# A product-key expert layer: half of its token tiles on gathered rows, half against streamed tables

## The chip, the core and the metric

One core of a Trainium2 chip runs the whole program. Its engines work side by side and meet at semaphores: TensorE (PE, the products), VectorE (DVE), ScalarE (ACT), GpSimd (POOL) and SyncE (SP, which only issues transfers here); 16 DMA engines move the data. The metric is the device time of one execution in microseconds (us), the median of several runs.

## What is computed

A decoder block over 1024 tokens of width 1024, all in float32: attention (stick-breaking and sliding-window heads), then an expert layer with 16,384 experts. Each token picks 16 experts for each of 8 heads, 128 in all, and gets a sum of rows of `v`, weighted by a gate times a gelu of the dot product with the same rows of `u`:

```python
cand = (v1[..., :, None] + v2[..., None, :]).reshape(T, PEER_HEADS, PEER_TOPK * PEER_TOPK)
top_s, pos = lax.top_k(cand, PEER_TOPK)
idx = jnp.take_along_axis(cand_idx, pos, axis=-1)
gate = jax.nn.softmax(top_s, axis=-1)
h = jax.nn.gelu(jnp.einsum('cd,chkd->chk', xc, u[ic]))
return jnp.einsum('chk,chkd->cd', (gc * h).astype(v.dtype), v[ic])
```

`u` and `v` are 64 MiB each. A final normalisation follows.

## The kernel before

The 1024 tokens are 8 tiles of 128. The attention stages come first, with statically written loops; the change leaves them as they are. Then `experts` runs. `KeyScores` multiplies the normalised tokens (`x2_t`, stored transposed) with `w_q` and the keys, in two passes: tiles 0 and 1, then the other six; `evacuate` copies the scores out on ACT and SP stores them. DVE routes a tile (`pick_half_first` to `pick_gates`: two rounds of the best 8, on 16 sides of 128 scores and then on 8 tables of 256, the rows' numbers, the softmax), which gives 128 row numbers and gates for each token.

POOL then gathers: each indirect transfer (L1063) brings one 4 KB row for each of the 128 tokens, 512 KiB, into one of 8 slots for `u` or 8 for `v`. It stages 8 row numbers at a time (L1055). POOL's order is written out: the 128 gathers of `u` for tile 0; then, for each tile, groups of 8 of `v` for this tile and 8 of `u` for the next in turn; at the end the `v` rows of tile 7 alone. DVE takes the dot product of each gathered `u` row with its token (`dot_group`, L1197), 128 in a tile, with a part of the next tile's routing after every 16; `weigh` makes the weights. ACT turns each column of weights into a diagonal matrix (L1335), and PE multiplies it with the gathered `v` rows (`group`, L1372): two products of 512 columns for each gather. In tile 7 one `v` row in eight is added by DVE (`extra`). `finish` adds the residual and normalises.

Every engine runs its own list in order. A gather waits for its slot; a dot product or a product waits for its gather.

## Time and profile before

| | us |
|---|---|
| median of 3 runs | 4010.37 |
| lowest, highest | 4006.89, 4012.83 |
| the profiled execution (its span, first to last instruction) | 4053.9 |

The page gives busy time by engine, the chain of work that ended last, and groups of instructions by source line. Matrix products appear as MATMUL records; in float32 each product of the program leaves two records (the 128 products of 512 columns of L775 are 256 records). PEld is the load of the stationary operand.

### The profile page before, as it was taken

What the parts mean: (1) busy time and instruction counts of PE and PEld (TensorE: products, weight loads), DVE (VectorE), ACT (ScalarE), POOL (GpSimd) and SP (SyncE); (2) the same over time, 40 slices, a digit from 0 to 9 for tenths busy, and PEclk for the clock granted to TensorE, in tenths of its full rate; (3) what the DMA queues carried; (4) which work ended last, traced back from release to release, by engine and by line L of the source; (5) the groups of instructions that cost most, each with busy time, mean ns of one, the idle gap of its engine ahead of it and who ended that gap; (6) DMA issues with size and microseconds to landing.
All of it is one profiled execution on the core that took longest, in us unless ns stands there. A gap on an engine that the chain in (4) does not pass through costs nothing.

```text
span 4053.9 us, 36202 instructions
## 1 busy us (share of the span) xinstructions
PE 2946.8 (73%) x8280; PEld 1429.7 (35%) x8280; DVE 2097.3 (52%) x4538; ACT 704.7 (17%) x1566; POOL 2393.8 (59%) x2391
## 2 busy tenths in 40 slices
PE   8998978899056776666666676666766667666699
PEld 4655564566022232222222232222322223222243
DVE  1007872258856555654665465556645654444411
ACT  1116632111011111111111111111111111111122
POOL 1001004116777777777777777777777777777765
PEclk8999999999577888778887887878888788888899
DMA  3000012558899999999999999999999999999998
GB/s 104 32 0 1 1 47 85 166 167 298 286 369 324 358 370 348 347 348 360 354 357 346 370 345 348 353 374 334 353 351 381 335 343 356 365 354 356 354 334 304
DMA packets 352122, 1153.17 MB, mean 284 GB/s; under 512 B 36240, under 2 KB 80272, under 8 KB 351120
## 3 DMA queue, kind: packets, MB, share of 16 engines
q0 software_dynamic: 294912, 1073.87, 71.6%
q1 hardware_dynamic: 57104, 78.14, 5.6%
q8 instruction: 36, 0.59, 0.1%
q14 instruction: 70, 0.57, 0.0%
HBM read 1130.90 MB, written 20.97 MB: 284 GB/s over the span
## 4 chain that ended last, share of the span: by engine, by line
issue 27%; POOL 27%; PE 12%; DVE 8%; DMA 6%; POOLq 2%; DVEq 0%; ACT 0%; another core or an unknown queue 0%; SPq 0%; ACTq 0%
POOL ex_u L1063 14%; POOL ex_v L1063 11%; PE ex_acc L1372 10%; DMA ex_u<-in_peer_u,ex_index_u 4%; DMA ex_v<-in_peer_v,ex_index_v 2%; DVE ex_prod L1197 2%; PE kl_q L874 2%; DVE bias L1197 1%; POOL ex_index_v L1055 1%; DVE ex_left L1115 1%; DVE ex_half_i L1114 1%; POOLq L993 1%; DVE ex_half_v L1111 1%; POOLq L994 1%; POOL ex_index_u L1055 0%
## 5 line engine op out<-in xcount | busy, mean ns | idle before, releaser
L1372 PE MATMUL ex_acc<-ex_v,ex_diag 128*128 128x512 f32 x4032 | 2017.0, 664 | 1007.4 <-DMA ex_v<-in_peer_v,ex_index_v 768.5
L1372 PEld LDWEIGHTS ex_acc<-ex_v,ex_diag 128*128 128x128 f32 x4032 | 854.8, 215 | 2168.9 <-issue 2160.9
L1063 POOL DMA_INDIRECT ex_u<-in_peer_u,ex_index_u x1024 | 1114.3, 1088 | 385.4 <-issue 318.5
L1063 POOL DMA_INDIRECT ex_v<-in_peer_v,ex_index_v x1024 | 1066.7, 1042 | 414.5 <-issue 306.2
L1197 DVE CUSTOM_DVE_ANT_0 ex_prod<-ex_u,ex_x 128x1024 f32<-128x1024 f32 x512 | 628.7, 1228 | 1008.7 <-DMA ex_u<-in_peer_u,ex_index_u 878.2
L1335 ACT ACTIVATE ex_diag<-ident,ex_wt 128x128 f32<-128x128 f32 x1008 | 398.1, 401 | 2242.4 <-PE ex_acc L1372 1517.9
L1197 DVE CUSTOM_DVE_ANT_0 bias<-ex_u,ex_x 128x1024 f32<-128x1024 f32 x512 | 628.8, 1228 | 80.6 <-DMA ex_u<-in_peer_u,ex_index_u 53.2
L874 PE MATMUL kl_q<-x_t,ex_v 128*128 128x256 f32 (+1 forms) x768 | 228.3, 450 | 0.8 <-DVE keys_t L1254 0.8
L468 POOL TENSOR_SCALAR_AFFINE_SELECT st_sp<-st_sp 128x1024 f32<-128x1024 f32 x8 | 8.7, 1090 | 362.4 <-DVE st_sp L422 362.4
L252 PE MATMUL pj_acc<-x_t,pj_w 128*128 128x512 f32 x384 | 167.4, 599 | 1.3 <-DVE x_t L207 1.3
L874 PEld LDWEIGHTS kl_q<-x_t,ex_v 128*128 128x128 f32 x768 | 142.3, 190 | 66.4 <-issue 53.6
L415 DVE SCALAR_TENSOR_TENSOR x_t<-st_zs 128x1024 f32<-128x1024 f32 x36 | 45.4, 1262 | 142.6 <-ACT st_zs L371 142.4
L775 PE MATMUL mx_y<-qk_t,mx_mt 128*128 128x512 f32 x256 | 114.4, 605 | 3.7 <-ACT mx_mt L706 3.7
L252 PEld LDWEIGHTS pj_acc<-x_t,pj_w 128*128 128x128 f32 x384 | 73.7, 192 | 94.0 <-issue 92.3
L754 POOL TENSOR_TENSOR mx_hs<-mx_hs,minus_half 128x16 f32<-128x16 f32 x8 | 23.2, 2905 | 137.3 <-DMA mx_g<-in_norm_g 131.1
L325 PE MATMUL st_c<-st_sp,tri 128*128 128x512 f32 x144 | 79.4, 644 | 9.3 <-POOL st_sp L468 8.1
L1197 DVE DVE_READ_ACCUMULATOR2_ANT ex_dots<- 128x1 f32 x1024 | 84.1, 82 | 0.0
L1068 POOL TENSOR_TENSOR ex_index_ut<-ex_index,ex_zero_i 128x128 int32<-128x128 int32 x8 | 7.8, 979 | 126.7 <-DVEq L1189 124.3
L224 DVE COPY pj_w_twice<-pj_w 128x1024 f32<-128x1024 f32 x2 | 1.3, 690 | 145.9 <-DMA pj_w<-in_w_in 145.9
L775 PEld LDWEIGHTS mx_y<-qk_t,mx_mt 128*128 128x128 f32 x256 | 48.9, 194 | 64.5 <-issue 58.8
L249 PE MATMUL pj_acc<-pj_w,x_t 128*128 128x256 f32 (+1 forms) x384 | 69.9, 344 | 0.0
L1055 POOL TENSOR_TENSOR ex_index_v<-ex_index_vt,ex_zero_i 128x8 int32<-128x8 int32 x128 | 60.2, 470 | 11.9 <-PE ex_acc L1372 5.7
(162 smaller groups left out, 1930.2 us busy)
## 6 DMA issues: line engine op xcount, KB each, us to landing
ex_v<-in_peer_w_q SPq DMA_DIRECT2D x16, 1024.0 KB, 5.8
ex_u<-in_peer_u,ex_index_u POOLq DMA_INDIRECT x1024
ex_v<-in_peer_v,ex_index_v POOLq DMA_INDIRECT x1024
pj_w<-in_w_in SPq DMA_DIRECT2D x9, 1024.0 KB, 5.8
x_scratch<-mx_x SPq DMA_DIRECT2D x16, 512.0 KB, 2.7
ex_x<-x_scratch SPq DMA_DIRECT2D x16, 512.0 KB
ex_sc<-score_scratch SPq DMA_DIRECT2D x7, 1024.0 KB
mixed<-in_x SPq DMA_DIRECT2D x8, 512.0 KB, 4.1
```

The lines of the kernel that those rows point to most:

```text
L249: last = nc.tensor.matmul(acc[:, n % 4, 0:at[1]], h_t[:, c, part * P:(part + 1) * P], slot[:, c, at[0]:at[0] + at[1]], **st)
L252: last = nc.tensor.matmul(acc[:, n % 4, :], slot[:, c, at:at + P], h_t[:, c, part * HALF:(part + 1) * HALF], **st)
L325: last = nc.tensor.matmul(csum[:, cols], tri[:], soft[:, n % 3, cols], start=True, stop=kb == i)
L415: nc.vector.scalar_tensor_tensor(out=lsp[:, n % 2, :], in0=zs[:, n % 4, :], scalar=-1.0, in1=zs[:, n % 4, :], op0=ALU.mult, op1=ALU.max).t ...
L775: last = nc.tensor.matmul(y[:, t % 2, hf * HALF:(hf + 1) * HALF], m_t[:, t % 2, c, :], w[:, c, hf * HALF:(hf + 1) * HALF], start=c == 0, s ...
L874: last = self.nc.tensor.matmul(self.q[:, n % 2, 0:tiles * P], self.w[:, g % self.ring, c, (b % 2) * P:(b % 2 + 1) * P], self.x2_t[:, c, fi ...
L993: engine.wait_ge(signal, value)
L1055: nc.gpsimd.tensor_tensor(stage[:, half, :], tile_index[:, bass.ds(j * RG, RG)], zero_i[:, 0:RG], ALU.add).then_inc(ready, 1)
L1063: nc.gpsimd.indirect_dma_start(out=ring[:, k, :], out_offset=None, in_=table, in_offset=bass.IndirectOffsetOnAxis(ap=stage[:, half, k:k + ...
L1197: nc.vector.tensor_tensor_reduce(out=prod[k % 2][:], in0=u[:, k, :], in1=x2[:], scale=1.0, scalar=0.0, op0=ALU.mult, op1=ALU.add, accum_ou ...
L1335: nc.scalar.activation(diag[:, k, :], ident[:], ACT.Copy, scale=wt[:, bass.ds(j * RG + k, 1)]).then_inc(diag_ready, 1)
L1372: ins = nc.tensor.matmul(acc[:, hf * HALF:(hf + 1) * HALF], diag[:, k, :], v[:, k, hf * HALF:(hf + 1) * HALF], start=first and k == 0, sto ...
```

## The change

Tiles 0, 5, 6 and 7 (`PICKED`) keep gathered rows. Tiles 1 to 4 (`DENSE`) are computed against all 16,384 experts:

- `u`, laid out in advance as 128 chunks of 128 experts, transposed (`peer_ut`, a copy of the input in another order), and `v` are streamed by SP: for each chunk 512 KiB of each. `hidden` forms all dot products of a chunk with the live dense tiles (8 products of 128 columns for each live tile, in one instruction each); ACT applies gelu; `gated` multiplies with the gates on DVE; `values` multiplies with `v` (for each live tile 8 products of 512 columns in 4 chunks); `add` adds the result to a total in SBUF.
- The gates of a dense tile must be a full 128 experts by 128 tokens table for each chunk. `one_hots` (DVE) writes for four tokens the two one-hot patterns of their row numbers, `scale_ones` (4 ACT instructions) scales one by the gates, `build` (4 PE products of 128 columns) multiplies them, `read_gates` (ACT) copies the table out; there are 32 such batches for a tile. The table is stored to DRAM in rows of 512 bytes and loaded again, once per four chunks.
- The gathered tiles have 4 slots for `u` and 6 for `v`. The diagonals go. POOL's `spread` puts a token's 128 weights into one column of a 32-column operand otherwise zero, and `take` multiplies it with the 128 `v` rows of that token: four tokens at a time, in four column groups of 32, two halves of 512 columns, 8 products for 4 gathers. A `v` gather now brings the 128 rows of one token (so `index_v` is turned on PE).
- `schedule()` writes out 257 steps with work. A step has one chunk for the dense tiles that are live, and with it a number of dots, takes, routing pieces and gate batches. Routing is cut into 61 or 63 pieces, each of which waits for the one before it. The order in which tiles are routed is 0, 1, 2, 5, 3, 4, 6, 7.
- Nothing loops any more in this stage: all engines' lists are written out.

The diff, cut to its core:

```diff
+CHUNKS = 128
+SUB = 32
+BATCH = 4
+BLOCK = 4
+PICKED = [0, 5, 6, 7]
+DENSE = [1, 2, 3, 4]
+ROUTED = [0, 1, 2, 5, 3, 4, 6, 7]
...
+def schedule():
...
+        rate = {0: 2, 1: 2, 2: 2 if whole_team else 1, 3: 3 if whole_team else 2, 4: 4}
...
+        for _ in range(rate[n]):
+            g, at = dots // P, dots % P
+            if g >= len(PICKED) or k < routed_at.get(g, 1 << 30) + 2:
+                break
+            if at == 0 and g >= 1 and k < ended[g - 1] + 2:
+                break
+            if g >= 1 and at >= 10 and before[1] - 32 * (g - 1) <= (at - 10) // 4:
+                break
+            dots += 1
+            left -= 1.33
+            if at == P - 1:
+                ended[g] = k
+                break
+        s.dots = (first, dots)
+        start = taken
...
+        for _ in range(2 if n >= 3 else 1):
+            g, at = taken // 32, taken % 32
+            if g >= len(PICKED) or g not in ended or k < ended[g] + 4:
+                break
+            if g + 1 < len(PICKED) and before[0] - P * (g + 1) <= 4 * at + 2:
+                break
+            taken += 1
+        s.take = (start, taken)
...
-        u = sb("ex_u", [P, RG, D])
-        v = sb("ex_v", [P, RG, D])
-        diag = sb("ex_diag", [P, RG, P])
+        u = sb("ex_u", [P, RING, CH, NK])
+        v = sb("ex_v", [P, 2, GROUP, HALF])
+        a = sb("ex_a", [P, 2 * GROUP, ND * P])
+        gb = sb("ex_gb", [P, 2, ND * SUBS, BLOCK * SUB])
+        stage = sb("ex_stage", [P, CHUNKS, SUB])
...
+        stage = sb("ex_stage", [P, CHUNKS, SUB])
...
+        ru = sb("ex_ru", [P, USLOTS, D])
+        rv = sb("ex_rv", [P, VSLOTS, D])
...
+                def load_u(k):
+                    if k >= RING:
+                        sp.wait_ge(h_ready, k - RING + 1)
+                    sp.dma_start(u[:, k % RING, :, :], peer_ut[k % CHUNKS]).then_inc(u_in[k % RING], 16)
+
+                def load_v(b, half):
+                    if b >= 1:
+                        sp.wait_ge(v_done, half_done(b - 1, half))
+                    sp.dma_start(v[:, half, :, :], v_blocks[b % (CHUNKS // GROUP), half]).then_inc(v_in[half], 16)
...
+                def row_of_u(g, n):
+                    if n == 0:
+                        pool.wait_ge(picked, ROUTED.index(PICKED[g]) + 1)
+                    at = g * P + n
+                    if at >= USLOTS:
+                        pool.wait_ge(dot_done, at - USLOTS + 1)
+                    nc.gpsimd.indirect_dma_start(
+                        out=ru[:, at % USLOTS, :], out_offset=None, in_=peer_u,
+                        in_offset=bass.IndirectOffsetOnAxis(ap=index_u[:, g % 2, n:n + 1], axis=0)).then_inc(
+                            ru_full[at % USLOTS], 16)
+
...
+                def spread(g, q):
+                    at = g * 8 + q
+                    if q == 0:
+                        pool.wait_ge(wt_read, g + 1)
+                    if at >= 2:
+                        pool.wait_ge(taken, 4 * (at - 1))
+                    for i in range(4):
+                        n = 4 * q + i
+                        column = wt[:].rearrange("p (j s) -> p j s", s=32)[:, :, n:n + 1]
+                        last = nc.gpsimd.tensor_tensor(wm[:, at % 2, i], bcast(column, [P, 4, 32]),
+                                                       bcast(unit[:, 31 - n:63 - n].unsqueeze(1), [P, 4, 32]), ALU.mult)
+                    last.then_inc(wm_ready, 1)
+
+                def row_of_v(g, n):
+                    at = g * P + n
+                    if n == 0:
+                        pool.wait_ge(picks_read, ROUTED.index(PICKED[g]) + 1)
+                    if at >= VSLOTS:
+                        pool.wait_ge(taken, (at - VSLOTS) // 4 + 1)
+                    token = n % 4 * 32 + n // 4
+                    nc.gpsimd.indirect_dma_start(
+                        out=rv[:, at % VSLOTS, :], out_offset=None, in_=peer_v,
+                        in_offset=bass.IndirectOffsetOnAxis(ap=index_v[:, g, token:token + 1], axis=0)).then_inc(
+                            rv_full[at % VSLOTS], 16)
...
+                pool.wait_ge(ks.s_ready, UNITS)
+                for g in range(NG):
+                    for n in range(P):
+                        if n == 4 and g >= 1:
+                            root(PICKED[g - 1])
+                        if n % 16 == 0:
+                            spread(g, n // 16)
+                        row_of_v(g, n)
+                        if g + 1 < NG and n + USLOTS < P:
+                            row_of_u(g + 1, n + USLOTS)
+                        if g + 2 < NG and n + USLOTS >= P:
+                            row_of_u(g + 2, n + USLOTS - P)
...
+                def one_hots(d, i):
+                    b = d * BATCHES + i
+                    if i == 0:
+                        dve.wait_ge(picks_read, ROUTED.index(DENSE[d]) + 1)
+                    if b >= 2:
+                        dve.wait_ge(gp_full, b - 1)
+                    at = i * BATCH
+                    nc.vector.tensor_tensor(oh[:, b % 2, :, :, :],
+                                            bcast(iota[:].unsqueeze(1).unsqueeze(1), [P, 2, BATCH, NK]),
+                                            bcast(tr[:, d % 2, 0:2, at:at + BATCH].unsqueeze(3), [P, 2, BATCH, NK]),
+                                            ALU.is_equal).then_inc(oh_ready, 1)
...
+                def gated(k):
+                    lo, hi = live(k)
+                    b, c = k // GROUP, k % GROUP
+                    dve.wait_ge(gelu_done, k + 1)
+                    dve.wait_ge(gb_in[b % 2], 16 * (b // 2 + 1))
+                    if k >= 2 * GROUP:
+                        dve.wait_ge(v_done, half_done(b - 2, 1))
+                    cols = slice(lo * P, hi * P)
+                    nc.vector.tensor_tensor(a[:, k % (2 * GROUP), cols].rearrange("p (s t) -> p s t", t=SUB),
+                                            act_h[:, k % 2, cols].rearrange("p (s t) -> p s t", t=SUB),
+                                            gb[:, b % 2, lo * SUBS:hi * SUBS, c * SUB:(c + 1) * SUB],
+                                            ALU.mult).then_inc(a_ready, 1)
+
+                def add(n, half, d):
+                    dve.wait_ge(v_done, n + 1)
+                    if n == 0:
+                        dve.wait_ge(sums_in, 16 * ND)
+                    dest = total_of(d)[:, 4 * half:4 * half + 4, :]
+                    nc.vector.tensor_tensor(dest, whole(vp[:, n % 2, :]), dest, ALU.add).then_inc(added, 1)
...
+                for k in range(MORE):
+                    route(0, k)
+                for k in range(PIECES):
+                    route(1, k)
+                    if k == 4:
+                        move_index(0)
+                    if k % 6 == 5 and k >= 11:
+                        dot((k - 11) // 6) if k < 58 else None
+                for i in range(BATCHES):
+                    one_hots(0, i)
+                    for k in (2 * i, 2 * i + 1):
+                        if k < PIECES:
+                            route(2, k)
+                    if i % 2 == 1:
+                        dot(8 + i // 2)
+                for i in range(BATCHES):
+                    one_hots(1, i)
+                    dot(24 + i)
...
+                gated(0)
+                for k, s in enumerate(steps):
+                    if k >= 1:
+                        for n, b, half, d in values_at(k - 1):
+                            add(n, half, d)
+                    for g in s.done:
+                        add_rows(g)
+                    for g in s.weigh:
+                        weigh(g)
+                    for g in s.moved:
+                        move_index(g)
+                    for d, i in s.ones:
+                        one_hots(d, i)
+                    for at in range(*s.dots):
+                        dot(at)
+                    for n, piece in s.route:
+                        route(n, piece)
+                    if k >= 1:
+                        for t in [PICKED[g] for g in steps[k - 1].done] + [DENSE[d] for d in steps[k - 1].dense_done]:
+                            mean(t)
+                    if k >= 3:
+                        for g in steps[k - 3].done:
+                            scale(PICKED[g], x1[:], gf[:])
+                        for d in steps[k - 3].dense_done:
+                            scale(DENSE[d], total_of(d), whole(gf[:]))
+                    if k + 1 < TOTAL:
+                        gated(k + 1)
...
-                    for k in range(slots):
-                        pe.wait_ge(v_full[k], 16 * (t * GROUPS + j + 1))
-                        pe.wait_ge(diag_ready, at + k + 1)
-                        for hf in range(2):
-                            ins = nc.tensor.matmul(acc[:, hf * HALF:(hf + 1) * HALF], diag[:, k, :],
-                                                   v[:, k, hf * HALF:(hf + 1) * HALF],
-                                                   start=first and k == 0, stop=last and k == slots - 1)
-                        ins.then_inc(v_free, 1)
...
+                def hidden(k):
+                    lo, hi = live(k)
+                    cols = slice(lo * P, hi * P)
+                    at = slice((DENSE[0] + lo) * P, (DENSE[0] + hi) * P)
+                    pe.wait_ge(u_in[k % RING], 16 * (k // RING + 1))
+                    if k >= 2:
+                        pe.wait_ge(gelu_done, k - 1)
+                    for c in range(CH):
+                        last = nc.tensor.matmul(hp[:, k % 2, cols], u[:, k % RING, c, :], x2_t[:, c, at],
+                                                start=c == 0, stop=c == CH - 1)
+                    last.then_inc(h_ready, 1)
+
+                def values(n, b, half, d):
+                    if half == 0:
+                        pe.wait_ge(a_ready, GROUP * (b + 1))
+                    pe.wait_ge(v_in[half], 16 * (b + 1))
+                    if n >= 2:
+                        pe.wait_ge(added, n - 1)
+                    for c in range(GROUP):
+                        last = nc.tensor.matmul(vp[:, n % 2, :], a[:, (b * GROUP + c) % (2 * GROUP), d * P:(d + 1) * P],
+                                                v[:, half, c, :], start=c == 0, stop=c == GROUP - 1)
+                    last.then_inc(v_done, 1)
+
+                def take(n):
+                    g, s = n // 32, n % 32
+                    pe.wait_ge(wm_ready, 8 * g + s // 4 + 1)
+                    if s == 0 and g >= 1:
+                        pe.wait_ge(y_squared, turn_of[PICKED[g - 1]] + 1)
+                    for hf in range(2):
+                        for j in range(4):
+                            at = 4 * n + j
+                            if hf == 0:
+                                pe.wait_ge(rv_full[at % VSLOTS], 16 * (at // VSLOTS + 1))
+                            last = nc.tensor.matmul(gacc[32 * j:32 * j + 32, hf * HALF:(hf + 1) * HALF],
+                                                    wm[:, n // 4 % 2, n % 4, j, :],
+                                                    rv[:, at % VSLOTS, hf * HALF:(hf + 1) * HALF],
+                                                    start=s == 0, stop=s == 31, skip_group_check=True)
+                    last.then_inc(taken, 1)
...
+                turn_picks(ROUTED[0])
+                for d in range(BUILT_FIRST):
+                    turn_picks(DENSE[d])
+                    for i in range(BATCHES):
+                        build(d, i)
+                pe.wait_ge(ks.s_read, UNITS)
+                hidden(0)
+                for k, s in enumerate(steps):
+                    if k + 1 < TOTAL:
+                        hidden(k + 1)
+                    for t in s.turn:
+                        turn_picks(t)
+                    if k >= 1:
+                        for g in steps[k - 1].weigh:
+                            turn_weights(g)
+                    for d, i in s.build:
+                        build(d, i)
+                    for n in range(*s.take):
+                        take(n)
+                    for n, b, half, d in values_at(k):
+                        values(n, b, half, d)
...
+            a = _np.ascontiguousarray(a.reshape(CHUNKS, P, CH, P).transpose(0, 3, 2, 1))
```

## Rows read from the trace of the kernel before

**Rows 1.** The page: span and engines' busy shares.

```profile
span 4053.9 us, 36202 instructions
...
PE 2946.8 (73%) x8280; PEld 1429.7 (35%) x8280; DVE 2097.3 (52%) x4538; ACT 704.7 (17%) x1566; POOL 2393.8 (59%) x2391
```

**Rows 2.** Stage windows: busy us (x) per engine, PEclk, DMA share, GB/s.

```profile
800.00:1000.00 200.00, 199.50 (x793) 134.29 (x792) 139.01 (x470) 34.60 (x85) 72.23 (x64) 1.00 0.69 233
...
1700.00:2100.00 400.00, 270.24 (x539) 114.16 (x538) 224.36 (x521) 53.38 (x136) 294.83 (x301) 0.83 0.95 354
```

**Rows 3.** The page: the chain that ended last, by engine.

```profile
issue 27%; POOL 27%; PE 12%; DVE 8%; DMA 6%; POOLq 2%; DVEq 0%; ACT 0%; another core or an unknown queue 0%; SPq 0%; ACTq 0%
```

**Rows 4.** The page's groups: count, busy, mean ns, idle before, releaser.

```profile
L1372 PE MATMUL ex_acc<-ex_v,ex_diag 128*128 128x512 f32 x4032 | 2017.0, 664 | 1007.4 <-DMA ex_v<-in_peer_v,ex_index_v 768.5
...
L1063 POOL DMA_INDIRECT ex_u<-in_peer_u,ex_index_u x1024 | 1114.3, 1088 | 385.4 <-issue 318.5
...
L1335 ACT ACTIVATE ex_diag<-ident,ex_wt 128x128 f32<-128x128 f32 x1008 | 398.1, 401 | 2242.4 <-PE ex_acc L1372 1517.9
```

**Rows 5.** Timeline (start, us, engine, line): gathers, TensorE after a wait.

```profile
2014.17 0.94 POOL L1063 DMA_INDIRECT ex_v<-in_peer_v,ex_index_v  x1 [0.30 <-issue]
...
2014.79 15.79 PE L1372 MATMUL ex_acc<-ex_v,ex_diag 128*128 128x512 f32 x32 [14.54 <-DMA ex_v<-in_peer_v,ex_index_v]
...
2015.80 0.34 PEld L1372 LDWEIGHTS ex_acc<-ex_v,ex_diag 128*128 128x128 f32 x1 [0.52 <-issue]
2016.65 0.34 PEld L1372 LDWEIGHTS ex_acc<-ex_v,ex_diag 128*128 128x128 f32 x1 [0.52 <-issue]
```

**Rows 6.** A window before any gather: 512-byte score rows stored.

```profile
850.00:880.00 30.00, 29.50 (x120) 19.65 (x119) 28.39 (x86) 5.41 (x13) 0.00 (x0) 1.00 0.23 66
```

**Rows 7.** Timeline, key scores: products of 256, 128 and 512 columns.

```profile
781.33 3.62 PE L874 MATMUL kl_q<-x_t,ex_v 128*128 128x256 f32 x16
...
784.79 0.61 PE L884 MATMUL kl_s<-keys_t,kl_qt 128*128 128x128 f32 x4
...
832.03 7.03 PE L874 MATMUL kl_q<-x_t,ex_v 128*128 128x512 f32 x16
```

**Rows 8.** Timeline, stick-breaking stage: 64-column products, then what follows them.

```profile
401.21 1.09 PE L339 MATMUL st_o<-x_t,sb_v 128*64 128x128 f32 x16
402.23 1.16 PE L308 MATMUL st_z<-qk_t 64*128 64x128 f32 x16
```

**Rows 9.** Timeline: the first gather and its first reader.

```profile
885.78 1.20 POOL L1063 DMA_INDIRECT ex_u<-in_peer_u,ex_index_u  x1 [0.98 <-POOL ex_index_u L1055]
...
890.83 1.23 DVE L1197 CUSTOM_DVE_ANT_0 ex_prod<-ex_u,ex_x 128x1024 f32<-128x1024 f32 x1 [7.44 <-DMA ex_u<-in_peer_u,ex_index_u]
```

**Rows 10.** Groups after 820 us by shape: DVE, ACT and POOL.

```profile
L1239 DVE TENSOR_TENSOR ex_y<-ex_acc,ex_x 128x1024 f32<-128x1024 f32 x7 | 8.6, 1225 | 3.7 <-DVE ex_wt L1218 2.8 <-issue 0.9
...
L856 ACT ACTIVATE kl_out<-kl_s 128x512 f32<-128x512 f32 x16 | 9.6, 597 | 8.3 <-PE kl_s L884 6.3 <-issue 2.0
...
L1068 POOL TENSOR_TENSOR ex_index_ut<-ex_index,ex_zero_i 128x128 int32<-128x128 int32 x8 | 7.8, 979 | 126.7 <-DVEq L1189 124.3 <-issue 1.4 <-POOL ex_index_vt L1068 1.0
```

**Rows 11.** Timeline of tile 0's routing on DVE: three of its groups.

```profile
843.33 0.87 DVE L1120 MAX8 ex_half_v<-ex_left 128x8 f32<-128x128 f32 x4
...
846.08 2.77 DVE L1129 TENSOR_TENSOR ex_cand<-ex_half_v 128x256 f32<-128x256 f32 x8
...
883.10 0.29 DVE L1186 TENSOR_TENSOR ex_gates<-ex_gate_e,ex_gsum 128x128 f32<-128x128 f32 x1
```

**Rows 12.** Key scores: first and last start of products and early copies.

```profile
L874 PE MATMUL kl_q<-x_t,ex_v x725: 379/379/595, 779.8 to 1018.2; 128*128 128x256 f32 x118, 128*128 128x512 f32 x64
...
L853 ACT ACTIVATE ex_sc<-kl_s x15: 272/277/277, 781.5 to 839.6; 128x128 f32<-128x128 f32 x15
```

**Rows 13.** Timeline of the end: last sum and store.

```profile
4044.38 1.23 DVE L1239 TENSOR_TENSOR ex_y<-ex_acc,bias 128x1024 f32<-128x1024 f32 x1 [2.12 <-PE ex_acc L1372]
...
4050.87 0.34 SPq L1040 DMA_DIRECT2D out<-ex_y  x1
```

946 lines of the change are left out of this document (566 added, 380 removed).

## Prediction

> **What bounds the kernel now.** I read the page first for the shares of the whole span: no engine is full, PE 73%, POOL 59%, DVE 52% [rows 1]. The stage windows say why: the key scores end at about 1019 us with PE full, and from 1300 to 3700 us every window looks like the one shown, the DMA engines at 0.95 of their time and 354 GB/s, POOL at 295 of 400 us, PE at 270, DVE at 224 [rows 2]. The chain agrees: 27% POOL and 27% "issue" against 12% PE and 8% DVE [rows 3]. The group of gathers has 1.09 us busy and 0.38 us idle each, mostly issue, 1.46 together [rows 4]; alone an issue is 0.94 + 0.30 = 1.24 us [rows 5], so it is the transfers that set 1.46: 512 KiB in 1.46 us is 359 GB/s. 2048 gathers at 1.46 are 2990 us of the 4054. All else hides under them. The clock of PE is 0.83 in that stage [rows 2] because it waits some 14.5 us and then starts at the lower level, 0.85 us from one weight load to the next [rows 5] where full speed has 0.44.
>
> **What goes.** 1024 of 2048 gathers: 537 MB, at 1.46 us some 1495 us of DMA time. With them half of the dots (512 x 1.23 us), all 1008 diagonals and the staging. All of that but the gathers is hidden.
>
> **What comes, and what it costs alone.** Stepping through `schedule()`, the dense tiles join at chunks 0, 0, 64 and 88, so the tables are streamed for 216 chunks: 226 MB, plus 67 MB of gates out and in, in rows of 512 bytes. The one window with such rows and little else moves 66 GB/s at a share of 0.23, 287 at a full share [rows 6], against 354/0.95 = 373 for 4 KB rows.
>
> PE's full-speed prices: 16 records of 512 columns take 7.03 us, so a product is 0.87 us; of 256 columns 0.45 or less; of 128 0.22 [rows 7]. A dense tile costs 8 x 0.217 + 2 x 0.867 = 3.47 us in each chunk; 512 tile-chunks are 1775 us of PE. At four live tiles a step is 13.9 us, at three 10.4, at two 6.9, at one 3.5.
>
> The take is the unknown. The trace shows no 32-column groups, only groups of 64: 8 products of 128 columns (16 records) start 1.02 us ahead of what follows them, some 0.13 each with the changes of form at both ends, where a full-width one has 0.22 [rows 8]. So two run at once. If four do, a take is 2 x 0.87 + 0.2 = 1.9 us; if two, 3.7; if none, 7.1. I take 1.9, by the row with column groups, and keep the others as rivals.
>
> The Trainium skill, "TensorEngine Tiling (Array Packing)", section "Theoretical Speedup", gives up to 2 for groups of 64 and up to 4 for groups of 32. The row agrees with the first; nothing here shows the second. By the Trainium skill's figure a take would be 1.9 us, by a limit of two 3.7.
>
> DVE: a dot 1.23 us, an add over 512 columns of PSUM 0.61 (half of the 1.225 for 1024), a one-hot batch (1024 elements) 1.2 [rows 9, 10]. Routing: from the cut of 4 sides at 843.33 to the table at 846.08 are two pieces and a cast, and from there to the gates 37.3 us [rows 11]. Each of the 61 pieces adds a wait of about 0.15: some 66 us a tile, 1.08 a piece.
>
> A gather's slot: from issue to reader 5.05 us with nothing queued [rows 9]. POOL's product for `spread` has 0.98 us for 128x128 as nearest row [rows 10], so 1 us in each take; below nothing is excluded, since it is an added instruction.
>
> **The sum, by stages.**
>
> Start. The key scores end at 1019 us as before [rows 12]; the early scores are there at 840, tile 0 is routed by about 890. Then tile 1's routing stops at piece 4, in `move_index(0)`: it waits for a transpose that PE does behind all key scores. That is the first lost stretch. From 1020: 56 pieces and 8 dots, 72 us; tile 2's routing with 32 one-hot batches and 16 dots, 132; 32 batches with a dot each, 86 (DVE 2.5 us a batch, ACT about 2.5: four scalings at 0.40 [rows 4] and a read of 512 columns at 0.6 [rows 10]). The last table's store and load, 15. The steps begin at 1325 us. DMA engines and PE stand nearly idle for 300 us.
>
> Steps 0 to 63, two tiles: PE 6.9, DVE 1.2 + 4 x 1.08 + 0.6 + 0.35 and waits of 0.5, 7.2. In 20 of them two gate batches bring PE to 8.7. 44 x 7.3 + 20 x 8.9 = 500.
>
> Steps 64 to 87, three tiles, 24 batches, 11 takes: 250 + 21 + 21 of PE, and 20 for steps in which DVE is longer: 312.
>
> Steps 88 to 127, four tiles, a take and four dots: PE 13.9 + 1.9 = 15.8. DMA: 8 gathers (4.2 MB) and 1.05 MB at 373 GB/s are 14.1, gates 0.9: 15.0, at the share of 0.95 15.8 too. Two limits at once; I take 16.4 for 38 steps: 655.
>
> Steps 128 to 191, two tiles, two dots and half a take: PE 7.9; DMA 3.15 MB and gates 8.9, at 0.95 9.4. DVE's rows must come two steps ahead, so I take 9.7: 621.
>
> Steps 192 to 215, one tile: PE 4.4, DMA 8.6/0.95 = 9.1, taken as 9.4: 226. Steps 216 to 221, gathers alone at 1.46 and `spread`: 38.
>
> Steps 222 to 256: 32 takes with nothing beside them. Six slots hold a take of four rows and two more; rows seven and eight are issued when a take ends: 0.2 + 1.24 to the second issue + 5 to its landing + 1.7 us of products (3.4 at the lower clock, which TensorE has after a wait, as in [rows 5]) = 8.1 to 9.8. At 9.0, and 14 to get the weights across: 302. The gathers alone would need 5.8.
>
> End: from the last sum to the last store were 6.5 us plus the store [rows 13]; now five tiles are finished there: 22.
>
> 1325 + 500 + 312 + 655 + 621 + 226 + 38 + 302 + 22 = 4001 us, against 4053.9: 53 less. The profiled execution is 1.1% above the median; 4001 less 1.1% is 3958. **So 1495 us of gathers are removed, and nearly all of it comes back**: about 300 in a start that is serial on DVE, 200 and more of streaming, and a stage of four tiles at PE's pace.
>
> **The rivals.**
>
> Slots too few (slower). In the stage with four tiles a take frees four `v` slots, and eight gathers of 1.4 us follow it in POOL's order; DVE, in order, stands at the dot of the fourth row, and with it the gated products and adds behind it. It decides from the point at which those gathers, beside the streams, take longer than a step: 15.8 of 16.4 us is my estimate of both. For it: the DMA share of 0.95 in the window [rows 2]. Against: 10 us of slack between a take and the next dot. Price: 2.2 us in 40 steps, 1.5 in 88, 1 in the last 32, 10 us at the start: 262 us, which gives 4263, as a run 4217.
>
> Two column groups at a time, not four (slower): 1.8 us more in 37 + 11 takes, hidden under DMA in the next 88 steps, 1.8 in the last 32: 144, a run of 4101. None at a time: 5.2 x 80, and 64 x 0.9: 474, a run of 4427.
>
> All hides well (faster): streams and gathers mix without loss, so steps 88 to 127 take 15.8, the next 88 take 9.0, the last 32 take 7.5, and the first 64 follow PE. That is 25 + 62 + 50 + 15 = 150 less, a run of 3810. For it: POOL's 0.30 us between issues may shrink without the extra semaphore instructions, and at 1.24 it was not the limit.
>
> **How the numbers follow.** My forecast 0.42, good hiding 0.20, slots 0.20, two groups 0.13, none 0.05. The likeliest case has its own range of 3890 to 4030, a fifth of which lies above 4002. The range reaches from 3800 to 4190: below it lies half of the good case, above it half of the slots' and the serial take. About 0.2% (8 us) is what a measurement here can tell. Faster: 0.20 + 0.42 x 0.78 = 0.53; same 0.05; slower 0.42.
>
> **What would show it.** The start: DVE's wait of about 100 us before 1019, and a first `hidden` product followed by a gap until 1325. The take: 16 records in 1.9 or 3.7 us. The stage with four tiles: step of 16.4 us, PE's share above 0.93 and clock near 1.0; were it DVE waiting on `ex_ru` and PE's share below 0.88, the slots rival is right. Steps 128 to 215: a DMA share at 0.9 or more with PE at 0.8 and then 0.5. The last takes: one in 9 us at 230 GB/s. The prediction is wrong if a resource that I left out sets the step, ACT above all (at four tiles it has only 0.6 us of gelu and so should be free), or if the written-out lists cost time of their own.

## The result, and the profile after

| | us |
|---|---|
| before, median of 19 runs (lowest, highest) | 4016.64 (4006.89, 4026.63) |
| after, median of 19 runs (lowest, highest) | 4007.39 (3996.77, 4020.39) |
| ratio, 95% interval | 0.9974, 0.9964 to 0.9985 |
| the profiled execution of after, its span | 4014.06, 4012.3 |

The changed kernel is 0.26% faster; the interval lies below 1, but by little. The forecast was 3958 us, 1.3% faster. The page of after, with span, busy shares, PE's 40 slices and its clock, the two large queues, the chain by engine, and four groups:

```profile
span 4012.3 us, 34704 instructions
...
PE 3402.4 (85%) x12844; PEld 1867.3 (47%) x12844; DVE 1787.3 (45%) x3894; ACT 639.9 (16%) x1413; POOL 1275.5 (32%) x1232
...
PE   7998978899257999899889999999998999665554
...
PEclk8999988999655999999999999999999999887776
...
q0 software_dynamic: 147456, 536.94, 37.2%
q1 hardware_dynamic: 268656, 369.67, 26.8%
...
PE 52%; DMA 18%; DVE 6%; POOL 2%; issue 2%; ACT 1%; SPq 0%; DVEq 0%; ACTq 0%; POOLq 0%
...
L1750 PE MATMUL ex_hp<-x_t,ex_u 128*128 128x256 f32 (+3 forms) x3456 | 938.4, 426 | 52.0 <-DMA ex_u<-in_peer_ut 52.0
L1761 PE MATMUL ex_vp<-ex_v,ex_a 128*128 128x512 f32 x2048 | 932.3, 602 | 3.2 <-DVE x_t L1536 2.5
...
L1340 POOL DMA_INDIRECT ex_rv<-in_peer_v,ex_index_v x512 | 526.7, 1029 | 528.9 <-PE ex_gacc L1775 402.7
L1775 PE MATMUL ex_gacc<-ex_rv,keys_t 128*32 128x512 f32 x2048 | 458.3, 729 | 257.2 <-DMA ex_rv<-in_peer_v,ex_index_v 256.7
```

PE has risen from 73% to 85% and POOL has fallen from 59% to 32% [rows 1]; the chain, which was 27% POOL and 27% "issue" [rows 3], is now 52% PE and 18% DMA. PE's slices have two thin places, one a quarter of the way in (2, 5) and one at the end (6 6 5 5 5 4). The windows by stage (start:end, length, then busy us and count for PE, PEld, DVE, ACT and POOL, PE's clock, DMA share, GB/s) put numbers on them:

```profile
1020.00:1100.00 80.00, 9.96 (x49) 8.54 (x47) 72.81 (x261) 6.86 (x20) 9.17 (x9) 0.54 0.37 110
1100.00:1240.00 140.00, 85.23 (x335) 74.14 (x334) 128.64 (x292) 75.64 (x211) 37.31 (x27) 0.50 0.58 177
1340.00:1840.00 500.00, 470.42 (x1780) 317.46 (x1779) 356.16 (x997) 104.29 (x274) 65.80 (x64) 0.99 0.69 235
1840.00:2160.00 320.00, 283.09 (x977) 145.95 (x976) 191.35 (x475) 55.62 (x146) 117.36 (x110) 0.95 0.79 279
2160.00:2800.00 640.00, 631.07 (x1892) 257.74 (x1891) 283.02 (x471) 28.30 (x48) 353.29 (x347) 0.99 0.91 333
2800.00:3400.00 600.00, 553.21 (x2083) 315.87 (x2083) 221.45 (x389) 25.75 (x68) 301.34 (x285) 0.96 0.95 352
3700.00:4012.00 312.00, 173.75 (x460) 29.38 (x460) 7.97 (x11) 5.74 (x10) 117.98 (x141) 0.70 0.60 198
```

Before, one window stood for the whole stage, with the DMA engines at 0.95 and PE at 270 of 400 us [rows 2]. Now there are different limits one behind the other: DVE from 1020 on (73 of 80 us, 129 of 140), PE from 1340 to 2800 (631 of 640 with four tiles), to 3400 the DMA engines by their share (0.95), with PE close behind (553 of 600), and nothing at all in the last 312 us: PE 174, POOL 118, DMA 0.60.

### The profile page after: what moved, and what is told of

It is laid out like the page before. It is cut to its first block, busy times and chain, and to the rows that moved or that the text cites. A ratio compares the mean times of both kernels' runs of the same rounds, so it can differ in the third digit from the quotient of the medians.

```text
span 4012.3 us, 34704 instructions
## 1 busy us (share of the span) xinstructions
PE 3402.4 (85%) x12844; PEld 1867.3 (47%) x12844; DVE 1787.3 (45%) x3894; ACT 639.9 (16%) x1413; POOL 1275.5 (32%) x1232
## 2 busy tenths in 40 slices
DMA packets 416279, 908.82 MB, mean 227 GB/s; under 512 B 26096, under 2 KB 188912, under 8 KB 415216
## 4 chain that ended last, share of the span: by engine, by line
PE 52%; DMA 18%; DVE 6%; POOL 2%; issue 2%; ACT 1%; SPq 0%; DVEq 0%; ACTq 0%; POOLq 0%
PE ex_vp L1761 18%; PE ex_hp L1750 16%; DMA ex_rv<-in_peer_v,ex_index_v 9%; PE ex_gacc L1775 7%; PE ex_hp L876 6%; DMA ex_u<-in_peer_ut 5%; PE ex_gp L1738 3%; DMA gate_scratch<-ex_stage 2%; DVE ex_ru L1509 1%; POOL ex_rv L1340 1%; POOL ex_ru L1315 1%; DVE ex_oh L1496 1%; ACT ex_stage L1641 1%; PE ex_vp L886 1%; DMA ex_ru<-in_peer_u,ex_index_u 0%
## 5 line engine op out<-in xcount | busy, mean ns | idle before, releaser
L1315 POOL DMA_INDIRECT ex_ru<-in_peer_u,ex_index_u x512 | 585.9, 1144 | 1441.2 <-DVE ex_hid L1509 1195.0
L1750 PE MATMUL ex_hp<-x_t,ex_u 128*128 128x256 f32 (+3 forms) x3456 | 938.4, 426 | 52.0 <-DMA ex_u<-in_peer_ut 52.0
L1761 PE MATMUL ex_vp<-ex_v,ex_a 128*128 128x512 f32 x2048 | 932.3, 602 | 3.2 <-DVE x_t L1536 2.5
L1750 PEld LDWEIGHTS ex_hp<-x_t,ex_u 128*128 128x128 f32 x3456 | 641.8, 195 | 384.8 <-issue 225.3
L1509 DVE CUSTOM_DVE_ANT_0 ex_ru<-ex_ru,ex_x 128x1024 f32<-128x1024 f32 x512 | 619.1, 1229 | 270.6 <-DMA ex_ru<-in_peer_u,ex_index_u 255.6
L1340 POOL DMA_INDIRECT ex_rv<-in_peer_v,ex_index_v x512 | 526.7, 1029 | 528.9 <-PE ex_gacc L1775 402.7
L1775 PE MATMUL ex_gacc<-ex_rv,keys_t 128*32 128x512 f32 x2048 | 458.3, 729 | 257.2 <-DMA ex_rv<-in_peer_v,ex_index_v 256.7
L1761 PEld LDWEIGHTS ex_vp<-ex_v,ex_a 128*128 128x128 f32 x2048 | 383.8, 193 | 499.3 <-issue 485.0
L1775 PEld LDWEIGHTS ex_gacc<-ex_rv,keys_t 128*32 128x32 f32 x2048 | 82.5, 120 | 577.4 <-DMA ex_rv<-in_peer_v,ex_index_v 400.7
L1738 PE MATMUL ex_gp<-ex_oh 128*128 128x128 f32 x1024 | 204.1, 363 | 124.0 <-ACT ex_stage L1641 84.3
L876 PE MATMUL ex_hp<-x_t,ex_rv 128*128 128x256 f32 (+1 forms) x768 | 228.3, 450 | 0.8 <-DVE keys_t L1558 0.8
```

The lines of the kernel that those rows point to most:

```text
L876: last = self.nc.tensor.matmul(self.q[:, n % 2, 0:tiles * P], self.w[:, g % self.ring, c, (b % 2) * P:(b % 2 + 1) * P], self.x2_t[:, c, fi ...
L1315: nc.gpsimd.indirect_dma_start(out=ru[:, at % USLOTS, :], out_offset=None, in_=peer_u, in_offset=bass.IndirectOffsetOnAxis(ap=index_u[:, g ...
L1340: nc.gpsimd.indirect_dma_start(out=rv[:, at % VSLOTS, :], out_offset=None, in_=peer_v, in_offset=bass.IndirectOffsetOnAxis(ap=index_v[:, g ...
L1509: nc.vector.tensor_tensor_reduce(out=rows, in0=rows, in1=x2[:], scale=1.0, scalar=0.0, op0=ALU.mult, op1=ALU.add, accum_out=hid[:, g % 2, ...
L1738: last = nc.tensor.matmul(gp[:, j, :], oh[:, b % 2, 1, j, :], oh[:, b % 2, 0, j, :], start=True, stop=True)
L1750: last = nc.tensor.matmul(hp[:, k % 2, cols], u[:, k % RING, c, :], x2_t[:, c, at], start=c == 0, stop=c == CH - 1)
```

## The stages, forecast and measured

Stage times from the starts of the `hidden` products of each chunk and of the takes (L1750, L1775). The columns "after" and "repeat" are two profiled executions of the same kernel, 4012.3 and 4005.4 us.

| stage | forecast | after | repeat |
|---|---|---|---|
| up to the first `hidden` | 1325 | 1296.6 | 1296.8 |
| steps 0 to 63 | 500 | 505.7 | 507.5 |
| steps 64 to 87 | 312 | 333.3 | 335.2 |
| steps 88 to 127 | 655 | 638.6 | 633.0 |
| steps 128 to 191 | 621 | 604.4 | 599.7 |
| steps 192 to 214 | 217 (of 226 for 24) | 209.4 | 209.5 |
| from step 215 to the last store | 371 (9, 38, 302, 22) | 424.3 | 423.7 |
| span | 4001 | 4012.3 | 4005.4 |

The sum of spans was right within 11 us, in part by luck: the last stage and steps 0 to 87 came out 80 us longer than forecast, the others 69 us shorter. What made the forecast miss came behind the sum.

## The experiments

Ratios are to the kernel before on the same chip, with 95% intervals. The two kernels with short dots and the last one ran on another chip than the rest; the kernel before takes 4020.75 us there, against 4017.03 and 4018.65.

### The same two kernels again

Both kernels unchanged, to see how far one profiled execution stands for its kernel.

> The kernel before, unedited, to have its profiled execution beside its times. Theory one: the execution of 4053.9 us on which the sum of the prediction was built was itself an outlier of about 1% above this kernel's runs; then this one lies within 0.3% of the median, 4005 to 4030. Theory two: the profiler slows this kernel's gathers, in every profiled execution; then it is 4045 to 4060 again, while the times of the runs stay at 4010 to 4020.

> The changed kernel, unedited, on the same chip as the kernel before. Both theories: span of 4000 to 4020 and a ratio of 0.996 to 0.999. The stages should stay within 1%: 639 us for steps 88 to 127, 604 for 128 to 191.

Measured: before 4016.68 us (0.9999, 0.9987 to 1.0011), span 4013.1; after 4006.91 (0.9975, 0.9960 to 0.9991), span 4005.4. A run's time is its span plus some 1.8 us in both (4014.91 for 4013.1, 4007.15 for 4005.4). The execution of before that the prediction was made from, 4053.9 us, lies above all 19 runs of that kernel, of which the highest is 4026.63. Its windows compared with the second one's show a stage that ran 1.4% slower all along: from 1300 to 3500 us 354 against 359 GB/s, and 1458 gathers against 1478. So it was an unusual execution. The durations from which the sum was made are the same in both (a dot has 1.228 us in either, a gather alone 0.94), so taking 1.1% off it was the error.

### One term each

**Tile 0's row numbers moved later.** In tile 1's routing the copy of tile 0's row numbers stands at piece 49 instead of piece 4.

```diff
-                    if k == 4:
+                    if k == 49:
                         move_index(0)
```

> Edit: the row numbers of tile 0 are taken over (move_index(0)) after piece 49 of tile 1's routing instead of after piece 4. Theory: in the changed kernel DVE waits 91.6 us there for a transpose that PE does behind all key scores, and everything after it is a serial start. 45 pieces at 1.08 us and 7 dots then run before 1020 us: the first product of the steps comes 50 to 56 us earlier than 1297 us, and the whole is 50 to 56 us shorter than the changed kernel (4012 us in the profile), so about 3958. Rival: the start hides behind something later (the gate tables' stores, the streams) and less than 15 us are won.

Measured: 3958.35 us (0.9862, 0.9832 to 0.9891). DVE's timeline of after, with the wait in brackets; then of this kernel, and its window behind the key scores:

```profile
1023.77 0.29 DVE L1487 CAST ex_index_v<-ex_tp 128x128 int32<-128x128 f32 x1 [91.64 <-PE ex_tp L1720]
```

```profile
1024.07 1.22 DVE L1458 TENSOR_REDUCE ex_row<-ex_cand 128x64 f32<-128x1024 f32 x1 [40.49 <-PE ex_tp L1720]
...
1020.00:1100.00 80.00, 37.63 (x156) 32.44 (x154) 71.28 (x222) 30.31 (x87) 14.22 (x9) 0.54 0.44 131
```

The wait of 91.64 us is the one that the prediction named (about 100 us). 45 pieces of routing, 49 us at 1.08, now run inside it, and 40.49 us are left. PE has 38 us of gate products in the window in which it had 10, and the first `hidden` starts at 1248.8 instead of 1296.6: 48 us, which is the whole gain of 49.

**More slots for the last takes.** From tile 5 on, the `v` gathers have ten slots: the six, and four in `ex_stage`, which holds gates until the last dense tile has stored them. An excerpt:

```diff
+WIDE = 10
...
+        def slot_of(at):
+            if at < P:
+                return rv[:, at % VSLOTS, :], (rv_full[at % VSLOTS], at // VSLOTS + 1)
+            s = (at - P) % WIDE
+            before = (P - s + VSLOTS - 1) // VSLOTS if s < VSLOTS else 0
+            rows = rv[:, s, :] if s < VSLOTS else rows_more[:, s - VSLOTS, :]
+            return rows, (rv_full[s], before + (at - P) // WIDE + 1)
```

> Edit: from tile 5 on the v gathers have 10 slots, the 6 of before and 4 in the gate staging buffer, which is free by then. Theory: in the last 32 takes the period of 10.1 us is a loop (take ends, two gathers issued, 5.2 us to land, 3.4 us of products at the lower clock) that exists only because four rows of each take are not prefetched. With 10 slots it falls to the larger of POOL (4 x 1.24 us and 1.1 of spread, 6.1) and DMA (4 x 1.46, 5.8): 6.2 us, 125 us less in all; steps 88 to 215 within 10 us of the changed kernel's 639 + 604 + 209. Rival one: the period is set by PE at its lower clock, it stays above 8.5 and less than 50 us are won. Rival two: slots also hold up steps 88 to 215, which then shorten by 40 us or more.

Measured: 3848.78 us (0.9583, 0.9564 to 0.9602). First the timeline of after in its last takes, then one window of after and of this kernel, and the gathers of this kernel in it:

```profile
3808.92 0.94 POOL L1340 DMA_INDIRECT ex_rv<-in_peer_v,ex_index_v  x1 [5.09 <-PE ex_gacc L1775]
3810.16 0.94 POOL L1340 DMA_INDIRECT ex_rv<-in_peer_v,ex_index_v  x1 [0.30 <-issue]
...
3815.44 3.81 PE L1775 MATMUL ex_gacc<-ex_rv,keys_t 128*32 128x512 f32 x14 [0.92 <-DMA ex_rv<-in_peer_v,ex_index_v]
...
3819.04 0.94 POOL L1340 DMA_INDIRECT ex_rv<-in_peer_v,ex_index_v  x1 [5.46 <-PE ex_gacc L1775]
```

```profile
3700.00:3820.00 120.00, 71.30 (x192) 12.25 (x192) 0.00 (x0) 0.00 (x0) 47.28 (x55) 0.72 0.62 205
```

```profile
3700.00:3820.00 120.00, 101.60 (x358) 17.70 (x356) 0.00 (x0) 0.00 (x0) 92.94 (x111) 1.00 1.01 396
...
L1358 POOL DMA_INDIRECT ex_rv<-in_peer_v,ex_index_v x55 | 51.6, 939 | 16.3 <-issue 15.4 <-PE ex_gacc L1794 0.9
```

With six slots the loop closes on itself: the first issue at 3808.92 and the next at 3819.04 are 10.1 us apart, made of 1.24 to the second issue, 5.28 until its landing starts the products (3810.16 to 3815.44) and 3.60 from there to the next issue. With ten, the releaser of POOL's idle time is no longer `ex_gacc` but "issue", the DMA engines move 396 GB/s at a share of 1.01, PE is back at full clock, and the last 31 takes last 171.1 us instead of 313.7, 5.5 us each. That is 143 of the 158 us; 9 to 14 lie in steps 128 to 191. The expectation had 6.2 us a take and 125 us in all: it priced `spread` at 1.1 us a take, and the trace has 0.4 (four products of 0.4 us for four takes). In the window a gather comes every 1.32 us, and POOL's own list (0.94 and 0.30 a gather, 0.10 of `spread`) is as long; whether the transfers, at a share of 1.01, would allow less wasn't tried.

**Two column groups instead of four.** The rows j and j+2 of a take share a column group, so two rows' sums are added onto the other two's and only two groups are in use.

```diff
-                            last = nc.tensor.matmul(gacc[32 * j:32 * j + 32, hf * HALF:(hf + 1) * HALF],
+                            last = nc.tensor.matmul(gacc[32 * (j % 2):32 * (j % 2) + 32, hf * HALF:(hf + 1) * HALF],
```

> Edit: the four tokens of a take are put into two column groups of 32 instead of four, so two tokens share one group and their sums are mixed (not the reference's output). Theory: the changed kernel runs four groups at once (starts 7 ns apart), a take of 1.9 us at the full clock. With two groups it is 3.6: 48 takes beside three or four dense tiles cost 1.7 us more each, 80 us, steps 128 to 215 stay, and the last takes go from 10.1 to 11.8: 135 us in all. Rival: PE has slack in steps 88 to 127 (DMA sets them), and the increase there stays under 30 us.

Measured: 4145.31 us (1.0325, 1.0302 to 1.0349). Two takes in the stage with four tiles, of after and then of this kernel (start, us, engine, line, operation):

```profile
2410.35 1.92 PE L1775 MATMUL ex_gacc<-ex_rv,keys_t 128*32 128x512 f32 x16
2426.13 1.93 PE L1775 MATMUL ex_gacc<-ex_rv,keys_t 128*32 128x512 f32 x16
```

```profile
2403.00 3.63 PE L1775 MATMUL ex_gacc<-ex_rv,keys_t 128*32 128x512 f32 x16
2420.49 3.63 PE L1775 MATMUL ex_gacc<-ex_rv,keys_t 128*32 128x512 f32 x16
```

A take is 1.92 us and 3.63 us: four at once, and two. The step shown grows from 15.78 to 17.49 us, by 1.71, the whole difference of the take. Over steps 88 to 127 it is 52 us (690.8 for 638.6; 58 against the repeat) for 37 takes, 1.4 to 1.6 each, so in this stage PE sets the step nearly alone. In steps 128 to 191, with half a take each, 64 x 0.85 = 54 us more of PE cost only 7 (12 against the repeat): PE had about that much slack, and is now busy 641 of the 660 us from 2800 to 3460. In the last takes, with nothing beside them, the price is 45 us.

**A quarter of the streamed `u`.** After the first three chunks only 2 of the 8 parts of each chunk are loaded; the products read what lies in the other six.

```diff
+                    part = CH if k < RING else 2
-                    sp.dma_start(u[:, k % RING, :, :], peer_ut[k % CHUNKS]).then_inc(u_in[k % RING], 16)
+                    sp.dma_start(u[:, k % RING, 0:part, :], peer_ut[k % CHUNKS][:, 0:part, :]).then_inc(u_in[k % RING], 16)
```

> Edit: after the first three chunks each load of u brings only 2 of the 8 parts of a chunk (128 instead of 512 KiB), so the dense tiles' sums are not the reference's; every instruction and wait stays. Theory: steps 128 to 215 are bound by the DMA engines (share 0.95), so 393 KB less in a step at 373 GB/s save 1.05 us: step of 9.44 goes to 8.4, of 9.1 to 8.0, 90 us in all; steps 88 to 127 are bound by PE and stay within 8 us of 639. Rival: the steps are bound by the slots and the order of DVE and POOL, and less than 30 us are won.

Measured: 3954.62 us (0.9848, 0.9831 to 0.9865). Steps 128 to 191 take 571.3 us instead of 604.4 (599.7 in the repeat), steps 192 to 214 200.9 instead of 209.4, steps 88 to 127 630.4 instead of 638.6 (633.0). The window of steps 128 on:

```profile
2800.00:3400.00 600.00, 562.00 (x2190) 322.28 (x2189) 232.78 (x412) 27.03 (x73) 322.45 (x308) 0.96 0.91 328
```

Transfers alone as the bound would have given some 90 us; 50 came, 37 to 42 of them after step 128, with the DMA share down only from 0.95 to 0.91. So the transfers do set part of the pace after step 128, and something else stands close behind. PE is one such thing (562 of 600 us here), the dots, which hold the gathers (below), another.

### What bounded the kernel before

The prediction read the DMA share of 0.95 as the bound of before. Two kernels test that, and the trace shows the mechanism.

**Half the bytes.** The kernel before with gathers of 2 KB instead of 4 KB rows, in the same number. Dots, products and the extra row read that half twice, so the sums are of other data.

```diff
-                            out=ring[:, k, :], out_offset=None, in_=table,
+                            out=ring[:, k, 0:HALF], out_offset=None, in_=table.rearrange("e (h n) -> (e h) n", h=2),
...
-                        nc.vector.tensor_tensor_reduce(out=prod[k % 2][:], in0=u[:, k, :], in1=x2[:], scale=1.0, scalar=0.0,
+                        nc.vector.tensor_tensor_reduce(out=prod[k % 2][:].rearrange("p (h n) -> p h n", h=2), in0=u[:, k, 0:HALF].unsqueeze(1).to_broadcast([P, 2, HALF]), in1=x2[:].rearrange("p (h n) -> p h n", h=2), scale=1.0, scalar=0.0,
```

> The kernel before with gathers of half a row (2 KB instead of 4 KB, 128 rows as before); dots and products read the half row twice, so the number of instructions and their shapes stay and the output is not the reference's. It asks what bound the kernel before. Theory of the prediction: the transfers set 1.46 us for each gather; with half the bytes POOL's own list is left, 8 x 1.24 us and the staging of 8 row numbers, 0.47 + 0.81 + 0.3, so 1.40, and only 0.06 to 0.1 x 1800 = 100 to 190 us go: 3830 to 3910. Rival: POOL's issues were themselves held up by full rings (1.09 busy against 0.94) in a way that the sum does not show, and the time falls under 3800.

**Short dots.** The kernel before with every dot over 8 instead of 1024 columns.

```diff
-                        nc.vector.tensor_tensor_reduce(out=prod[k % 2][:], in0=u[:, k, :], in1=x2[:], scale=1.0, scalar=0.0,
+                        nc.vector.tensor_tensor_reduce(out=prod[k % 2][:, 0:8], in0=u[:, k, 0:8], in1=x2[:, 0:8], scale=1.0, scalar=0.0,
```

> The kernel before with dot products over 8 of 1024 columns (not the reference's output); every instruction and wait stays, only DVE's long operation with two inputs goes. It asks what sets the 1.49 us of a gather there, after half the bytes have saved nothing. Theory: POOL's own list does, and its gathers are held while DVE runs a dot: in the trace of the kernel before those with a dot over less than a tenth of their time have 0.97 us, those with one over more than half 1.20. Without the long dots the mean falls from 1.06 to 0.95-0.97, the period to 1.38 to 1.42 and the time by 0.08 to 0.1 x 2048 = 130 to 200 us: 3820 to 3890. Rival: the DMA engines set it (share 0.96), the period stays at 1.46 or more and less than 60 us go.

Measured: half the bytes 4158.6 us (1.035, 1.033 to 1.0369), slower; short dots 3773.42 (0.9383, 0.9366 to 0.94), 247 us faster. The window from 1300 to 3500 us and two of POOL's groups in it (count, busy us, mean ns, idle before, releasers), first of the second execution of before, then of half the bytes, then of short dots:

```profile
1300.00:3500.00 2200.00, 1497.59 (x2948) 632.15 (x2949) 1259.47 (x2870) 303.41 (x772) 1640.84 (x1674) 0.82 0.96 359
...
L1063 POOL DMA_INDIRECT ex_u<-in_peer_u,ex_index_u x736 | 784.1, 1065 | 274.9 <-issue 195.9 <-POOL ex_index_u L1055 74.4 <-PE ex_acc L1372 4.6
...
L1055 POOL TENSOR_TENSOR ex_index_v<-ex_index_vt,ex_zero_i 128x8 int32<-128x8 int32 x92 | 51.9, 564 | 4.6 <-POOL ex_index_ut L1068 3.1
```

```profile
1300.00:3500.00 2200.00, 1413.11 (x2785) 594.72 (x2784) 1206.60 (x2768) 286.65 (x728) 1674.38 (x1582) 0.81 0.60 173
...
L1063 POOL DMA_INDIRECT ex_u<-in_peer_u,ex_index_u x699 | 825.2, 1181 | 259.1 <-issue 185.1 <-POOL ex_index_u L1055 70.3 <-PE ex_acc L1372 3.7
...
L1055 POOL TENSOR_TENSOR ex_index_v<-ex_index_vt,ex_zero_i 128x8 int32<-128x8 int32 x88 | 65.3, 742 | 3.9 <-POOL ex_index_ut L1068 2.6
```

```profile
1300.00:3500.00 2200.00, 1631.00 (x3223) 688.38 (x3224) 492.85 (x2980) 330.73 (x840) 1588.95 (x1825) 0.85 1.01 391
...
L1063 POOL DMA_INDIRECT ex_u<-in_peer_u,ex_index_u x806 | 760.9, 944 | 301.3 <-issue 212.0 <-POOL ex_index_u L1055 80.8 <-PE ex_acc L1372 7.6
...
L1055 POOL TENSOR_TENSOR ex_index_v<-ex_index_vt,ex_zero_i 128x8 int32<-128x8 int32 x100 | 21.4, 214 | 4.8 <-PE ex_acc L1372 1.6 <-POOL ex_index_ut L1068 1.5
```

With half the bytes the DMA engines fall to 0.60 and nothing gets faster, and with short dots the same bytes move 6% faster, so the share of 0.95 was not the bound. Both results lie outside their expectations: half the bytes were to save 100 us or more, short dots 130 to 200. With short dots the gathers of `u` take 0.944 us instead of 1.065, and the staging product for `v` 0.214 instead of 0.564 (the one for `u` has 0.21 in both). In the second execution of before the hold can be seen directly (start, us, engine):

```profile
2118.93 0.95 POOL L1063 DMA_INDIRECT ex_u<-in_peer_u,ex_index_u  x1 [0.30 <-issue]
2120.00 1.23 DVE L1197 CUSTOM_DVE_ANT_0 ex_prod<-ex_u,ex_x 128x1024 f32<-128x1024 f32 x1 [12.66 <-DMA ex_u<-in_peer_u,ex_index_u]
2120.18 1.86 POOL L1063 DMA_INDIRECT ex_u<-in_peer_u,ex_index_u  x1 [0.30 <-issue]
```

The gather at 2120.18 is issued into a running dot and ends 0.81 us after the dot does (2122.04 and 2121.23). So do the others: of the 1478 gathers in the window some 350 start with more than 0.2 us of a dot still to go, and nearly all of them end 0.81 us after its end. A gather that starts in no dot has 0.94 us for the most part, even where a dot begins during it. The account closes. From 1300 to 3500 us there are 1478 gathers in before, one in 1.488 us, and 1612 with short dots, one in 1.365. Of the 0.123 us less, 0.100 are the gathers' own length (1.055 to 0.955 on average over `u` and `v`), 0.022 the staging, 0.00 the idle time between them. 2048 x 0.123 = 252 us; the gain is 247. With short dots the DMA share reads 1.01, at 391 GB/s, but POOL's idle time is still "issue" and its own staging, and its gathers are at the length of one alone; that the transfers are the bound then is possible and not shown.

The Trainium skill, "SBUF — State Buffer", section "SBUF: two separate sides", says that a VectorE instruction with two SBUF inputs and a GpSimd instruction that reads SBUF exclude each other for the length of the whole instruction. The trace agrees: a gather issued into a dot waits for the dot's end, as above, and on average this costs a gather 0.10 us here.

Half the bytes made the kernel slower by the same hold. Its dots last the same 1.228 us, and gathers issued into one again end 0.82 us after it; but they are issued earlier in it, with 0.22 us of a dot still to go on average over all gathers, against 0.15 in before. A gather has 1.127 us on average instead of 1.055, and the staging for `v` 0.742 instead of 0.564, which is together the 0.09 us by which a gather's period is longer in this window (1.576 for 1.488). Why gathers and dots fall together in this way when the rows land sooner wasn't looked into.

**Short dots in the changed kernel.** The same edit at L1509.

```diff
-                    rows = ru[:, at % USLOTS, :]
-                    nc.vector.tensor_tensor_reduce(out=rows, in0=rows, in1=x2[:], scale=1.0, scalar=0.0, op0=ALU.mult,
+                    rows = ru[:, at % USLOTS, 0:8]
+                    nc.vector.tensor_tensor_reduce(out=rows, in0=rows, in1=x2[:, 0:8], scale=1.0, scalar=0.0, op0=ALU.mult,
```

> The same edit in the changed kernel (dots over 8 columns, not the reference's output). Theory: steps 88 to 127 are bound by PE and steps 128 to 215 by the DMA engines, where 0.52 us of gathers' holding do not matter; 639 and 604 + 209 us stay within 10 and 25 us; only the start, which is serial on DVE, gets shorter, by 56 dots x 1.15 = 64 us less what ACT holds up, 30 to 64 us. Rival: DVE's waits for gathered rows and its dots hold the steps; then steps 88 to 215 get 60 us or more shorter.

Measured: 3930.57 us (0.9772, 0.9746 to 0.9797), 76 us less than the changed kernel on the other chip, and 82 by the spans (3923.0 for 4005.4). The window of steps 128 on:

```profile
2800.00:3400.00 600.00, 552.35 (x2216) 318.52 (x2215) 90.97 (x423) 27.37 (x75) 276.89 (x315) 0.98 1.00 381
```

By stages, against the repeat: 26 us in the start, which is DVE's; 9 in steps 0 to 63; 2 in steps 88 to 127, which are PE's; 32 in steps 128 to 191 and 7 in steps 192 to 214; 6 from there to the last takes; 1 in the last takes (312.5 us against 313.4), in which there are no dots. So steps 128 to 214, too, were held by dots and not by transfers alone: 352 GB/s became 381. Their 39 us are more than the theory's 25 and less than the rival's 60.

### Together, and a better schedule

**Both repairs.** The edits of the later row numbers and of the ten slots in one kernel.

> Both edits together: tile 0's row numbers taken over at piece 49, and 10 slots for v from tile 5 on. They lie in different stages, so the gains of 49 and 158 us should add up: 4007 - 49 - 158 = 3800, ratio to the kernel before 0.946. Rival: what the start gives is partly lost in the stage that the DMA engines bound (0.96 of their time), and it ends at 3815 or more.

Measured: 3795.75 us (0.9439, 0.9419 to 0.9460). The first `hidden` starts at 1246.0 and the last 31 takes last 172 us, as with each alone: the two gains add.

**Gathers brought forward.** As above, with two dots a step instead of one while two dense tiles are live.

```diff
-        rate = {0: 2, 1: 2, 2: 2 if whole_team else 1, 3: 3 if whole_team else 2, 4: 4}
+        rate = {0: 2, 1: 2, 2: 2, 3: 3 if whole_team else 2, 4: 4}
```

> Both winning edits and a third: two dots in a step, not one, while only two dense tiles are live (steps 0 to 71), so that the DMA engines, at 0.69 of their time there, do some of the gathers that later crowd steps 128 to 215 (0.96). By the rule of schedule() the third and fourth dense tile then join at 72 and 104 (not 64 and 88), the last dot is in step 202 (not 221), and 250 steps (not 269) are written. Theory: each stage costs its largest engine; the sum of the steps falls by some 75 us, a tenth to a third of it is lost in the early steps, where DVE is then the longest: 3720 to 3745 us. Rival: the early steps are as much bound by DVE as the late ones by DMA, and it stays within 15 us of 3796.

Measured: 3687.93 us (0.9167, 0.9151 to 0.9184), 108 us less than without the edit, against an expected 50 to 75. An early and a late window, of both repairs and then of this kernel:

```profile
1340.00:1840.00 500.00, 465.83 (x1747) 310.12 (x1747) 336.22 (x940) 112.77 (x304) 65.46 (x65) 0.98 0.66 225
3500.00:3680.00 180.00, 122.57 (x409) 31.33 (x409) 32.58 (x57) 2.85 (x8) 109.70 (x119) 0.86 0.86 312
```

```profile
1340.00:1840.00 500.00, 452.95 (x1769) 286.28 (x1768) 319.49 (x791) 81.15 (x220) 205.54 (x183) 0.96 0.88 317
3500.00:3680.00 180.00, 143.02 (x707) 61.05 (x705) 21.49 (x38) 10.21 (x26) 91.42 (x110) 0.94 0.95 368
```

In the early steps the DMA engines carry 317 instead of 225 GB/s. That isn't free: steps 0 to 63 take 551.3 us instead of 508.4, with 126 dots instead of 64 and 13 takes (25 us of PE) among them. The other dense tiles now join later, at other steps, and the tables are streamed for 232 chunks instead of 216 (925.63 MB in all against 908.82). It pays all the same: the last chunk's products end at 3620 instead of 3532 us, but the last take starts at 3660 instead of 3779, since the last tile's 32 takes now run beside dense chunks (3424 to 3660) and no longer alone. The expectation counted the evener load and not this. This is the fastest of the kernels run, 8.3% below the one before.

## Why the prediction was wrong, point by point

- **The conversion, the step that failed.** "The profiled execution is 1.1% above the median; 4001 less 1.1% is 3958." The sum is built from durations and limits that don't scale with one unusual execution, and its 53 us of gain are counted from that execution. Without that step the forecast is 4001 + 2 = 4003 us, against 4007.4 measured and 4016.6 before: the gain of 0.3% that came. That the sum itself was so near is luck in part, as the errors below, up to 35 us a term, cancel. The repeats of both kernels show it (4013.1 for 4053.9, and 4005.4 for 4012.3).
- **What bounds before, read wrongly.** Not "the transfers that set 1.46", but POOL's own list with its gathers held by dots: half the bytes and short dots show it. The group itself said so: 1.09 us busy where a gather alone has 0.94, and idle time put down to "issue", not to a wait. It did little harm to the sum, which took 1.46 us and the GB/s as measured with the dots there, but it hid what the dots cost, 247 us in before.
- **The start.** Mechanism right, 1296.6 against 1325 us, with the wait of 91.64 us in its place and DVE as the limit. Of the 28 us, 4 are the pieces and dots up to the first batch (at 1088.3), 16 tile 2's routing with the first 32 batches (116 us for 132), and 12 the last table's store and load, which the first `hidden` doesn't wait for; the second 32 batches took 89 us for 86. The store and load come behind it: the first gated product waits 17.1 us for them, within steps 0 to 63. "Nearly idle for 300 us" was wrong: PE is busy 9.96 of the first 80 us, but 85 of 140 from 1100 to 1240, at a clock of 0.50, with the DMA engines at 0.58.
- **Steps 0 to 63.** 506 against 500.
- **Steps 64 to 87.** 333 against 312: the gates' stores were priced at nothing. PE's waits in 1840 to 2160 us (waiting line, what for, total, times, longest) and the one store whose issue on SP's queue was long:

```profile
PE ex_gp L1738 <- ACT ex_stage L1641: 20.5, 12, 8.6
PE ex_hp L1750 <- DMA ex_u<-in_peer_ut: 13.9, 1, 13.9
...
2056.83 11.65 SPq L1223 DMA_DIRECT2D gate_scratch<-ex_stage  x1
...
2068.53 16.87 SPq L1202 DMA_DIRECT2D ex_u<-in_peer_ut  x2
```

  A gate product waits for ACT's copy into the staging buffer, and that copy, by the kernel's text, for the store of what lies there (20.5 us). And SP, in order, sits 11.65 us in the record of a 2 MB store, though the gates for it had been copied by 2038.9, after which the next `u` loads are issued late: PE waits 13.9 us once. The repeat has the same (20.8 us, 11.5, 14.3). These 34 us are more than the 21 missing; whether the 20 us forecast for steps in which DVE is longer were needed wasn't checked. Neither wait was taken away in an experiment, so this is read from the trace alone.
- **The take, 1.9 us.** Right: 1.92, and 3.63 for two groups. The Trainium skill, "TensorEngine Tiling (Array Packing)", section "Theoretical Speedup", gives a speedup of up to 4 for a small dimension of 32; the trace agrees.
- **Steps 88 to 127.** 15.97 us a step against 16.4, within 0.2 of the 15.8 forecast for PE alone. Of the "two limits at once" only PE's was real: the DMA share is 0.91, a quarter of `u` and short dots save 2 to 8 us there, and 1.71 us more of PE cost 1.4 to 1.7 us. The slots rival asked for a PE share below 0.88 and a DVE-bound step; PE has 0.99, and with ten slots the stage takes 634.5 us, as in the repeat.
- **Steps 128 to 214.** 604 and 209 against 621 and 217; 9.44 us a step for 9.7. Named as DMA-bound; they are partly so (a quarter of `u`: 37 to 42 us less) and partly held by the dots (39 us less). "PE at 0.8" was wrong: it is busy 0.92 of the time from 2800 to 3400.
- **The last takes.** The loop through six slots was right in its parts, its size was not: 10.1 us a take for 9.0, since landing (5.3 for 5.0) and the products at the lower clock (3.6 for 1.7 to 3.4) both came out above the forecast's range. The 31 periods took 313.7 us for 279, 35 more, the largest mis-sized term; 19 more lie between step 215 and the first of these takes (79.9 us for 9 + 38 + 14). There the takes come 13.4 to 17.3 us apart, where eight gathers at 1.46 would need 11.7: in the timeline PE waits up to 6.7 us for a `v` row while POOL waits up to 4.7 us for a dot. Short dots take 6 us of it away, and the rest stays open. These 54 and the 27 of steps 0 to 87 nearly cancelled, by luck, against the 69 forecast too many in the start and in steps 88 to 214.

The statement that nearly all of the removed 1495 us of gathers comes back was right: 9 us are left.

## What to carry to other kernels

Before a profiled time is scaled, compare its span with the spans of other runs; a sum built from durations needs no scaling, and one execution can stand 1% off. A DMA share of 0.95 doesn't prove a bound: look at the queue's issuer, and ask what on another engine lengthens its instructions. When a loop of buffers is left alone at the end of a kernel, its price is issue + landing + use over the slots that it has, so give it the buffers that others have done with, or work to run beside.

## What the runs showed of the hardware that was not expected

- An indirect gather on GpSimd that is issued while a dot of 1.23 us runs on VectorE ends 0.81 us after the dot; alone it has 0.94 us. Dots lengthen the gathers of before from 0.955 to 1.055 us on average, and the 8-column product that stages `v`'s row numbers from 0.214 to 0.564 us; 247 of 4020 us hang on it.
- Gathers of 4 KB rows with takes but no dots beside them reach 396 GB/s (one in 1.32 us, share 1.01); with dots beside them 359.
- Four float32 products in groups of 32 columns run at once: 8 of them over 512 columns in 1.92 us, and 3.63 us when only two groups are used.
- The record of one 2 MB store on SP's queue took 11.65 us with the DMA share at 1.01 (2057 to 2069 us), where the stores before it took 0.43 and 0.51; in the repeat it took 11.5.
